# A two-layer streaming encoder step on one core: the bias table spread from memory, a gate half moved ahead of the first scores, and mixer A's casts moved into mixer B's units

## The reference, cut to what matters

```
z = x @ w_in                       # q_A | k_A | v_A | c_q | c_kv | k_rope
q = rms_norm(c_q) @ w_uq           # per head 64 plain and 32 rotary features
q_rope = rope(q[..., 64:], pos)    # x1*cos - x2*sin | x2*cos + x1*sin
y_A = window attention(q_A, k_A, v_A) with a relative bias per head and sinks
o   = latent attention(q_lat, q_rope, c_kv, k_rope)      # mixer B
y_B = o @ w_uv
g = sigmoid(x @ w_gate + b_gate)
h = g[:1024] * (y_A @ w_proj_a) + g[1024:] * (y_B @ w_proj_b)
x = LN1(alpha * x + h @ w_out)
x = LN2(alpha * x + (gelu(conv3(x Wa)) * (x Wb)) @ w_down)
```

## Time and profile before

| | us |
|---|---|
| median of 3 runs | 1901.82 |
| lowest, highest | 1900.15, 1901.82 |
| the profiled execution, its own time | 1900.86 |
| its span, first to last instruction | 1899.1 |
| PE busy in the span | 1847.1 (97%) |
| DVE, ACT, POOL busy | 1014.7, 654.4, 541.0 |
| mean granted TensorE clock (1 is full) | 0.992 |

### The profile page before, as it was taken

The page is one execution under the profiler, slowest core; times in us unless marked ns, Lnnn a source line. Parts: engine busy times, 40 slices in busy tenths (PEclk is TensorE's granted clock), DMA queues, the critical chain, the costliest instruction groups (busy, mean ns, idle before and its releaser), DMA issues. The chain is left out here.

```text
span 1899.1 us, 31847 instructions
## 1 busy us (share of the span) xinstructions
PE 1847.1 (97%) x12458; PEld 1755.0 (92%) x12458; DVE 1014.7 (53%) x1597; ACT 654.4 (34%) x1381; POOL 541.0 (28%) x244
## 2 busy tenths in 40 slices
PE   8899999999999999999999999999999999999996
PEld 8877888899999999999998788889999999999995
DVE  3567544558854423443765865445697443234447
ACT  4135333532433212332332443334334332132323
POOL 2321211133143234332422311112322333433331
PEclk9999999999999999999999999999999999999998
DMA  6443233232122122121241613323311211222121
GB/s 183 141 140 82 90 110 99 93 129 83 45 92 80 50 89 89 66 72 56 88 135 56 171 47 126 104 69 132 117 68 67 89 55 67 77 89 81 49 74 56
DMA packets 67875, 171.19 MB, mean 90 GB/s; under 512 B 16360, under 2 KB 34456, under 8 KB 60056
## 3 DMA queue, kind: packets, MB, share of 16 engines
q1 hardware_dynamic: 67768, 169.71, 27.6%
HBM read 150.90 MB, written 19.59 MB: 90 GB/s over the span
## 5 line engine op out<-in xcount | busy, mean ns | idle before, releaser
L704 POOL TENSOR_TENSOR w_lo<-w_raw,w_hi 128x1024 fp32r<-128x1024 f32 (+2 forms) x230 | 530.7, 2316 | 1285.8 <-ACT w_hi L791 1266.6
L791 ACT ACTIVATE w_hi<-w_raw 128x1024 fp32r<-128x1024 f32 (+2 forms) x228 | 218.2, 975 | 463.3 <-PE ps L1625 427.1
L1625 PE MATMUL ps<-x_hi,w_hi 128*128 128x320 f32 x1408 | 322.0, 310 | 4.0 <-POOL w_lo L704 4.0
L1625 PE MATMUL ps<-x_lo,w_hi 128*128 128x320 f32 x1408 | 321.3, 309 | 0.0
L1625 PE MATMUL ps<-x_hi,w_lo 128*128 128x320 f32 x1408 | 321.3, 309 | 0.0
L1625 PEld LDWEIGHTS ps<-x_hi,w_hi 128*128 128x128 f32 x1408 | 236.0, 188 | 4.6 <-issue 4.4
L1625 PEld LDWEIGHTS ps<-x_lo,w_hi 128*128 128x128 f32 x1408 | 235.9, 188 | 0.0
L1625 PEld LDWEIGHTS ps<-x_hi,w_lo 128*128 128x128 f32 x1408 | 235.9, 188 | 0.0
L1525 DVE TENSOR_SCALAR f_conv<-f_ext,vec 128x656 f32<-128x656 f32 x44 | 64.6, 1469 | 202.2 <-ACT tail L1016 199.7
L1892 PE MATMUL ps<-x_hi,w_hi 128*128 128x320 f32 x512 | 164.9, 322 | 0.0
L1892 PE MATMUL ps<-x_lo,w_hi 128*128 128x320 f32 x512 | 159.2, 311 | 0.0
(11 more groups left out here) (281 smaller groups left out, 3189.5 us busy)
## 6 DMA issues: line engine op xcount, KB each, us to landing
w_raw<-in_slabs SPq DMA_DIRECT2D x84, 1024.0 KB, 4.9
w_raw<-in_slabs SPq DMA_DIRECT2D x20, 768.0 KB, 4.1
gate_logits<-logits SPq DMA_DIRECT2D x64, 160.0 KB, 1.9
gates<-gate_logits SPq DMA_DIRECT2D x16, 640.0 KB, 6.2
w_raw<-in_slabs SPq DMA_DIRECT2D x16, 640.0 KB, 3.7
ckvc<-in_ckvc SPq DMA_DIRECT2D x16, 256.0 KB, 2.7
ckvc_t<-in_ckvc_t SPq DMA_DIRECT2D x16, 256.0 KB, 3.0
w_raw<-in_slabs SPq DMA_DIRECT2D x6, 512.0 KB, 5.9
```

The source lines that it names most:

```text
L704: pool.tensor_tensor(to, w_raw[:, s % 2, c], hi.bitcast(F32), ALU.subtract).then_inc(wlo_ready, 1)
L791: A(w_hi[:, s % 2, c], w_raw[:, s % 2, c], ACT.Copy).then_inc(whi_ready, 1)
L1625: ins = MM(out_[:, a, :], w, x[:, t, a * HT:(a + 1) * HT], start=t == 0 and w is wh and x is hi, stop=t == tiles - 1 and w is wl)
```

## The change

1. **The bias table.** SP stores the 8 x 384 table once to a scratch array in memory, 12 KB, and after the mask stores copies that array 128 times from memory to memory, one contiguous run of 12,288 bytes for each of 128 rows.
2. **The rotation.** The sine products are written back to PSUM in place, so each of the six operations has a PSUM operand; the sum comes first, then the difference, and the two jobs are counted taken behind them. `bias_p` is masked earlier, before job 22 is taken. TensorE runs two gate quarters before scores(0). SP stores the second rotated half first, and loads the caches of mixer A when job 29 is done, not taken.
3. **The casts.** ACT's high parts of y_A's tiles 0 to 2 are made behind units 19, 22 and 25, DVE's low parts behind `take_out` of these; the fourth after the last unit. The first projection of y_A becomes job 32 and runs before `J_UV`, now job 33; the first projection of y_B follows `J_UV` at once. Several arrays lie at other places in SBUF, `ya_lo` in place of `y_a`.

```
@@ SP, layer 0
                     sp.wait_ge(bias_tab, 1)
-                    sp.dma_start(bass.AP(table_dram.tensor, 0, [[REL, HEADS], [PITCH + 1, P], [1, REL]]),
-                                 tab_sb[:].unsqueeze(1).broadcast_to([HEADS, P, REL])).then_inc(table_stored, 16)
+                    sp.dma_start(tab_dram[:, :], tab_sb[:]).then_inc(table_once, 16)
                     sp.wait_ge(mask_made, 16)
...
+                    sp.wait_ge(table_once, 16)
+                    sp.dma_start(bass.AP(table_dram.tensor, 0, [[PITCH + 1, P], [1, PITCH]]),
+                                 tab_dram.rearrange("h n -> (h n)").unsqueeze(0).broadcast_to([P, PITCH])
+                                 ).then_inc(table_stored, 16)
...
-                sp.wait_ge(job_taken, layer * NJ + J_ROPE[1] + 2)
+                sp.wait_ge(job_done, layer * NJ + JC + J_ROPE[1] + 1)
...
-                for k in range(2):
-                    sp.wait_ge(qr_ready, layer * 2 + k + 1)
+                for k in (1, 0):
+                    sp.wait_ge(qr_ready, layer * 2 + 2 - k)
@@ ACT
+YA_HIGH = [B_FIRST + 3 + 3 * k for k in range(3)]
...
+                def ya_high(k):
+                    act.wait_ge(out_taken, layer * NU + AS_LAST + 1)
+                    A(ya_hi[:, k, :], y_a[:, k, :], ACT.Copy).then_inc(ya_hi_ready, 1)
...
+                    if u in YA_HIGH:
+                        ya_high(YA_HIGH.index(u))
+                ya_high(3)
                 for k in range(4):
-                    if k == 0:
-                        act.wait_ge(out_taken, layer * NU + NU)
-                    A(ya_hi[:, k, :], y_a[:, k, :], ACT.Copy).then_inc(ya_hi_ready, 1)
-                for k in range(4):
-                    act.wait_ge(job_taken, layer * NJ + J_UV + 2)
+                    act.wait_ge(uv_taken, layer + 1)
                     A(yb_hi[:, k, :], y_b[:, k, :], ACT.Copy).then_inc(yb_hi_ready, 1)
@@ DVE, the rotation
                 n0, n1 = J_ROPE
                 job(n0)
-                TT(halves(cqz[:, 0, :]), pair(n0), halves(cos_t[:]), ALU.mult)
-                TT(halves(cqz[:, 1, :]), pair(n0), halves(sin_t[:]), ALU.mult).then_inc(job_taken, 1)
+                TT(halves(cqz[:, 0, :]), pair(n0), halves(cos_t[:]), ALU.mult).then_inc(rotating, 1)
+                dve.wait_ge(rotating, layer * 4 + 1)
+                TT(pair(n0), pair(n0), halves(sin_t[:]), ALU.mult).then_inc(rotating, 1)
                 job(n1)
...
+                TT(halves(cqz[:, 1, :]), pair(n1), halves(cos_t[:]), ALU.mult).then_inc(rotating, 1)
+                dve.wait_ge(rotating, layer * 4 + 3)
+                TT(pair(n1), pair(n1), halves(sin_t[:]), ALU.mult).then_inc(rotating, 1)
+                dve.wait_ge(rotating, layer * 4 + 4)
+                TT(halves(q_r[1][:]), pair(n0), halves(cqz[:, 1, :]), ALU.add).then_inc(qr_ready, 1)
+                dve.wait_ge(qr_ready, layer * 2 + 1)
+                dve.sem_inc(job_taken, 1)
+                TT(halves(q_r[0][:]), halves(cqz[:, 0, :]), pair(n1), ALU.subtract).then_inc(qr_ready, 1)
+                dve.wait_ge(qr_ready, layer * 2 + 2)
+                dve.sem_inc(job_taken, 1)
@@ DVE, behind take_out and after the last unit
+                    if u - 1 in YA_HIGH:
+                        ya_low(YA_HIGH.index(u - 1))
                 take_out(NU - 1)
...
+                ya_low(3)
+                job(J_UV)
+                dve.tensor_copy(y_b[:, :, SEQ:], ps[:, 2 * (J_UV % 4), :].rearrange("p (k n) -> p k n", k=4)
+                                ).then_inc(uv_taken, 1)
@@ PE
-                pe.wait_ge(job_taken, layer * NJ + J_ROPE[0] + 2)
-                scores(0)
                 gate_half(0)
                 gate_half(1)
                 pe.wait_ge(job_taken, layer * NJ + J_ROPE[1] + 2)
+                scores(0)
                 scores(1)
...
+                proj(0, 0)
                 pe.wait_ge(out_taken, layer * NU + NU)
...
+                proj(0, 1)
+                for j in range(1, KD):
+                    proj(j, 0)
+                    proj(j, 1)
```

More of the change, by code:

```diff
@@ L91, with proj_job @@
 JC = 3
+def proj_job(j, k):
+    return J_PROJ + 2 * j + k if j + k else J_FIRST
 def before_norm(job0, k):
@@ L273, in build @@
         first_lo = [place("first_lo%d" % k, at, [P, 1024], F32R) for k, at in enumerate((10 * T + 2048, 40 * T))]
[L275 to L283, removed]
+        h_hi = place("h_hi", 4 * T, [P, KD, T], F32R)
+        h_lo = place("h_lo", 12 * T, [P, KD, T], F32R)
+        ya_hi = place("ya_hi", 31 * T, [P, 4, T], F32R)
+        ya_lo = place("ya_lo", 0, [P, 4, T], F32R)
+        yb_hi = place("yb_hi", 20 * T, [P, 4, T], F32R)
+        yb_lo = place("yb_lo", 24 * T, [P, 4, T], F32R)
+        mix_a = place("mix_a", 28 * T, [P, T])
+        mix_b = place("mix_b", 29 * T, [P, T])
+        gates = place("gates", 35 * T, [P, 3, 2, T])
         x_in = place("x_in", 16 * T, [P, KD, T])
-        res = place("res", 16 * T, [P, KD, T])
+        res_of = [place("res_out", 20 * T, [P, KD, T]), place("res_down", 16 * T, [P, KD, T])]
         mean = place("mean", 34 * T, [P, T])
@@ L929, in square @@
                 def square(which, k):
+                    res = res_of[which]
                     base = layer * 2 + which
@@ L1291, in take_out, with ya_low @@
                     dve.tensor_copy(to, src).then_inc(out_taken, 1)
+                def ya_low(k):
+                    dve.wait_ge(ya_hi_ready, layer * 4 + k + 1)
+                    TT(ya_lo[:, k, :], y_a[:, k, :], ya_hi[:, k, :].bitcast(F32), ALU.subtract).then_inc(ya_lo_ready, 1)
                 dve.wait_ge(sinks_ready, layer * 2 + 2)
@@ L1311, in _ @@
                         take_out(u - 1)
+                    if u - 1 in YA_HIGH:
+                        ya_low(YA_HIGH.index(u - 1))
                 take_out(NU - 1)
-                for k in range(4):
-                    dve.wait_ge(ya_hi_ready, layer * 4 + k + 1)
-                    TT(ya_lo[:, k, :], y_a[:, k, :], ya_hi[:, k, :].bitcast(F32), ALU.subtract).then_inc(ya_lo_ready, 1)
-                take(J_UV, y_b[:, :, SEQ:], ps[:, 2 * (J_UV % 4), :].rearrange("p (k n) -> p k n", k=4))
+                ya_low(3)
+                job(J_UV)
+                dve.tensor_copy(y_b[:, :, SEQ:], ps[:, 2 * (J_UV % 4), :].rearrange("p (k n) -> p k n", k=4)
+                                ).then_inc(uv_taken, 1)
                 for k in range(4):
@@ L1388, in add_last @@
                 def add_last(which):
-                    base, c = layer * 2 + which, cols(0)
+                    base, c, res = layer * 2 + which, cols(0), res_of[which]
                     dve.wait_ge(shifted_h[0], base * 2 + 2)
@@ L1916, in _, with proj @@
                 values(NU - 1)
+                def proj(j, k):
+                    slab, half = divmod(j, 2)
+                    hi, lo, made = ((ya_hi, ya_lo, ya_lo_ready), (yb_hi, yb_lo, yb_lo_ready))[k]
+                    dense(proj_job(j, k), S_PROJ + slab, half * KD + 4 * k, 4, hi, lo, None if k else half,
+                          ready=(lambda t: pe.wait_ge(made, layer * 4 + t + 1)) if j == 0 else None)
+                proj(0, 0)
                 pe.wait_ge(out_taken, layer * NU + NU)
@@ L1926, in _ @@
                 ins.then_inc(job_done, 1)
-                for j in range(KD):
-                    k, half = divmod(j, 2)
-                    dense(J_PROJ + 2 * j, S_PROJ + k, half * KD, 4, ya_hi, ya_lo, half,
-                          ready=(lambda t: pe.wait_ge(ya_lo_ready, layer * 4 + t + 1)) if j == 0 else None)
-                    dense(J_PROJ + 2 * j + 1, S_PROJ + k, half * KD + 4, 4, yb_hi, yb_lo, None,
-                          ready=(lambda t: pe.wait_ge(yb_lo_ready, layer * 4 + t + 1)) if j == 0 else None)
+                proj(0, 1)
+                for j in range(1, KD):
+                    proj(j, 0)
+                    proj(j, 1)
                 def sums(which, job0, k):
+                    res = res_of[which]
                     base = layer * 2 + which
```

48 lines of the change are left out of this document (24 added, 24 removed).

## The result

| | before | after |
|---|---|---|
| median of the runs, us | 1901.09 (4 runs) | 1886.82 (4 runs) |
| lowest, highest | 1900.15, 1901.82 | 1885.35, 1887.02 |
| the profiled execution, its own time | 1900.86 | 1887.02 |
| its span | 1899.1 | 1885.2 |
| PE busy | 1847.1 (97%) | 1843.2 (98%) |

The ratio is 0.9924, with a 95% interval of 0.9911 to 0.9938: 14.3 us less, where 15.5 were forecast. The time is inside the range and 1.4 us above the forecast of 1885.4.

A forecast was written before the change was run, and what follows sets the result against it. PE, busy 97%, bounds the kernel; time comes from its idle stretches or low clock. Parts 1, 2 and 3 give 8.0 + 8.7 - 1.2 = 15.5 us off 1900.86, so 1885.4 us; 8-in-10 range 1881.5 to 1894.

The forecast's parts named there:

- layer 1's stretch: RMS sums to job 11: 16.2 us in layer 1 against 24.3 in layer 0, so part 1 gains 8.0 us.
- the dip at unit 17: In layer 1 before the change, a 0.33 us wait followed by clock 0.53 for 3 us; its absence only in the range.
- I take the old rate per engine on twice the engines, 17 us: Length of the table's memory-to-memory copy in layer 0: 17 us, so an end near 49 us.
- the deadline: Slab 4 must land by about 59 us; any copy end up to 55 us gives part 1's whole gain.
- SP waiting for the table until about 50 us: Sign that the prediction is right: in layer 0 SP waits for the table's copy until about 50 us.
- The first rival: The table's copy is no faster than the keep copy or the store, layer 0's stall stays: 1893.4 us; chance 0.15.
- the gate wait: PE's gate quarter waits for bank 7 behind exps(2): 0.6 us a layer lost, between 0 and 1.6.
- The slack at scores(2): Peaks(0) and its chain are ready 0.8 us before PE reaches scores(2), so the scores wait goes in both layers.
- part 3 loses 1.2 us over both layers: Behind the last unit, 7.2 us to y_B against 6.6 before, because UV's chain stands open for 2.5 us.
- the 1.7 us of idle there now left the clock alone: Argument against a clock fall in the new 2.5 us gap before y_B: the existing idle there caused none.
- The window at 0.5 behind UV: Sign that the prediction is wrong: a stretch of clock at 0.5 behind UV.
- the second rival: The clock falls in the new gap before y_B, 1.4 to 1.6 us in each layer: 1888.4 us; chance 0.17.

The follow-up runs named there:

- table_only: The kernel before with part 1 alone, the bias table stored once and copied from memory to memory: 1892.54 us, ratio 0.9959.
- scores_only: The kernel before with part 2 alone (rotation, memsets, two gate quarters, SP's waits): 1891.53 us, ratio 0.9950.
- old_order: The changed kernel with scores(0) ahead of the first two gate quarters again: 1888.30 us, ratio 0.9927.
- no_casts: The changed kernel with y_A's casts and the order behind the last unit as before: 1882.60 us, ratio 0.9905.
- uv_first: The changed kernel with UV ahead of y_A's first projection again, casts still in mixer B's units: 1879.38 us, ratio 0.9890.
- casts_only: The kernel before with part 3 alone (casts moved, y_A's first projection ahead of UV): 1905.36 us over ten runs, ratio 1.0021.
- uv_after_one: The changed kernel with UV between the first and second tile of y_A's first projection: 1878.88 us, ratio 0.9881.
- split_2_2: The changed kernel with y_A's first projection in twelve pairs: two before the last values, two before UV, eight behind: 1877.99 us, ratio 0.9876.

## Why the prediction was right, and where it was not

**Part 1, right in time, the copy's length mis-sized.** The 8.0 us read from layer 1's stretch were there: PE is busy 16.00 of 16 us at full clock, and `table_only` gained 9.0. Its profiled execution, 1891.40, is 9.5 under the profiled one of before, and of these 9.5 about 1.4 are the dip at unit 17, which is not in its trace. The step that failed is "I take the old rate per engine on twice the engines, 17 us". It took 7.9, near the lower bound of 7.4 that a slab load gave. The old rate was no rate of an engine: with the source in memory the old pattern took 11.8 us and not 34.4. The error cost nothing, since the deadline was loose, but the sign named for it, SP waiting for the table until about 50 us, was wrong by 10. The first rival (the copy no faster than 26 or 35 us) rested on that rate and on the keep copy's, and neither carried over. The prediction also called the keep copy the one memory-to-memory transfer of the trace; the profile has a second, `out_vc_keep`, 448 KB in 8.6 us. The Trainium skill's figure for an engine, which the prediction took from "DMA: Bandwidth & Descriptors", section "Specifications", and did not use, gave an estimate of 3.4 us. The 7.9 measured are more than twice that.

**Part 2, right in its mechanism.** The rotation's operations were forecast at 0.86 us from one to the next and came at 0.86 to 0.97; the wait of scores(2) and the half clock behind it went in both layers; the gate wait was forecast at 0.6 a layer and came at 0.63 and 0.85. The stretch from the latent queries to scores(3) takes 15.44 us in both layers after. The slack at scores(2) was forecast at 0.8 and is about 0.4. DVE's chain was right (unit 0 starts 6.07 us after the latent queries, 6.16 forecast); it was PE that came 0.5 us sooner, half of it because scores(0) and scores(1) now run as one: 1.09 us from their start to the next instruction, against 0.64 and 0.69 for the two apart. The forecast said that PE does the same work up to scores(2), and took the same time for granted. Alone, part 2 gained 10.0 against 8.7; its profiled execution gained 7.3, with layer 0's stall 1.6 us longer than before. Parts 1 and 2 together gained 18.3 against 16.7, 1.6 more. In the profiled executions it is 1.8 more, and 1.4 of it is again the dip at unit 17, which was in the range but not in the forecast.

**Part 3, the term that was mis-sized.** The idle time was right: 7.26 us from the last values to y_B against 7.2 forecast, with the gap at 2.51 in both layers, so 2 x (7.26 - 6.60) = 1.3 us lost where 1.2 were forecast. What failed is "part 3 loses 1.2 us over both layers", because it had no term for the clock. The argument was "the 1.7 us of idle there now left the clock alone"; behind the 2.5 us it fell. The window at 0.5 behind UV, which the prediction named as a sign of being wrong, is there: the clock is 0.50 from 1281 to 1284 us. This was the second rival, held at 0.17 and priced at 3.0 us; the loss is 1.46 + 1.56 = 3.0 us, so its price was right, and with a fall in 12 of 14 places its chance was too low. Part 3 cost 3.8 us alone and 4.2 in the whole. The forecast erred by some 3.0 us here and by 1.6 the other way in the two other parts, and the difference is the 1.4 us by which the result missed. The moved subtractions cost nothing, as forecast: each took 0.82 us.

The clock's falls did not only follow the gap's length. In the profiled execution of before it fell behind a wait of 0.33 us; there is one such dip in `scores_only`, one in `old_order` (0.51 from 209 to 212 us, behind a wait of 0.33), and none in the kernel after, `table_only`, `no_casts` or `uv_first`. Nor did the code around the gap decide it: gap and neighbourhood were the same in `casts_only` and in the kernel after, and the clock was 1.00 behind the one and 0.65 to 0.72 behind the other. The Trainium skill, "TensorE: Matmul & The Clock Gate", section "What's actually happening", calls the rise of the clock at a kernel's start run-variable. It says so of the rise; of the fall, the traces show what stands above.

What stays open: what decides whether the clock falls behind a given gap, whether the 3.8 us of `casts_only` are made of such falls in nearly every run, and why the stall of layer 0 differed by 2 us between kernels that share its code.

## What to carry to other kernels

Before work is moved off a critical stretch, look at what that work was covering: here y_A's casts and y_A's product stood by turns over a chain of copy, high part and low part, and with the casts gone and the product moved ahead of UV the chain stood open. The product that has a chain behind it goes first and an independent one behind it; here that order, with the same casts, was 7.4 us faster than the changed kernel, and cutting the cover in pieces gave 1.4 more. In this kernel a small table was spread faster from memory than from 8 partitions of SBUF, and an elementwise operation beside GpSimd's was faster with one operand in PSUM; both are worth a try elsewhere.

## What the runs showed that was not expected

- One and the same pattern of 1024 runs of 1536 bytes took 34.4 us out of 8 SBUF partitions and 11.8 out of memory. The rows outermost then gave 8.7 and runs of 12,288 bytes 7.9 us, 1536 KB at about 194 KB per us, memory to memory.
- A gap of 2.51 us on TensorE was followed by half clock in 12 of the 14 places traced, and by full clock in the two of `casts_only`. The price of such a gap is then its length, or its length and 1.46 to 1.62 us (y_B's first job takes 4.98 to 5.14 us there, and 3.52 in `uv_first`).
- The runs of the two fastest kernels lie closest together: 0.3 us from lowest to highest in `uv_after_one` and 0.2 in `split_2_2`, 1.7 in the kernel after and 3.8 in the ten of `casts_only`. The gap alone doesn't explain it, since `uv_first`, which has none, spreads over 1.5.
- A slow DMA also held the engine that issues: six issues of SP behind the store took 3.9 to 5.6 us each, and 0.4 to 0.7 in the kernel after.
